# Two squared-relu layers: four plain tiles, then blocks of four tiles computed as seven half-width products

## The reference, cut to what matters

```python
def sq_relu_mlp(h, w1, w2):          # h: 512 x 1024, w1: 1024 x 4096, w2: 4096 x 1024
    u = jax.nn.relu(h @ w1)
    return (u * u) @ w2

x = x + sq_relu_mlp(rmsnorm_2(x, norm_mlp[layer]), w_mlp1[layer], w_mlp2[layer])   # layer 0 and 1
```

## Time and profile before

| what | value |
|---|---|
| median of three runs | 2443.79 us (2443.28 to 2448.42) |
| span of the profiled execution | 2446.3 us |
| its own time outside the span | not listed; the third run is 2448.42 us |
| TensorE busy | 2390.1 us (98%), 11206 matmuls |
| VectorE, ScalarE, GpSimd busy | 1234.3, 962.0, 196.0 us |
| the first layer's up tiles begin | 1483 us |
| the second layer's | 2079 us |

### The profile page before, as it was taken

How to read it: one execution, slowest core, us unless ns; L and a number is a source line. 1 busy time by engine, 2 the same in 40 slices (tenths; PEclk the granted TensorE clock), 3 DMA queues, 4 the chain that set the end, 5 groups by cost and what they waited for, 6 DMA issues and landing times.

```text
span 2446.3 us, 28445 instructions
## 1 busy us (share of the span) xinstructions
PE 2390.1 (98%) x11206; PEld 1912.1 (78%) x11206; DVE 1234.3 (50%) x2012; ACT 962.0 (39%) x1613; POOL 196.0 (8%) x147
## 2 busy tenths in 40 slices
PE   8999999999999999999999999999999899999998
PEld 7888888777777788888887677888887677888887
DVE  5533436788654445433336855424435775532432
ACT  4323224455432334322323554313324785431432
POOL 0100100322102000100100200000001100000000
PEclk9999999999999999999999999999999999999999
DMA  4323323211222232323323113322232012333332
GB/s 144 104 87 103 98 88 102 77 52 52 70 69 72 63 108 81 101 80 110 95 83 99 59 53 103 104 94 95 95 96 64 29 46 80 97 101 95 95 95 70
DMA packets 66805, 208.50 MB, mean 85 GB/s; under 512 B 7408, under 2 KB 15856, under 8 KB 66416
## 3 DMA queue, kind: packets, MB, share of 16 engines
q1 hardware_dynamic: 66672, 206.68, 27.1%
HBM read 204.55 MB, written 2.10 MB: 84 GB/s over the span
## 4 chain that ended last, share of the span: by engine, by line
PE 90%; DVE 4%; ACT 3%; issue 2%; DMA 1%; POOL 0%; POOLq 0%; SPq 0%; ACTq 0%; DVEq 0%
PE bank L1842 26%; PE bank L1846 26%; PE bank L1844 26%; PE bank L2009 2%; PE bank L1971 1%; PE bank L2016 1%; PE bank L2000 1%; PE bank L2062 1%; ACT whi L2130 1%; PE bank L1917 1%; DVE wlo L2435 1%; PE bank L1913 1%; PE bank L1915 1%; DMA wraw<-in_stream 1%; PE bank L1936 1%
## 5 line engine op out<-in xcount | busy, mean ns | idle before, releaser
L2435 DVE TENSOR_TENSOR wlo<-wraw,whi 128x1024 fp32r<-128x1024 f32 (+5 forms) x436 | 487.9, 1122 | 541.9 <-ACT whi L2130 541.1
L1842 PE MATMUL bank<-hhi,whi 128*128 128x512 f32 x1736 | 693.2, 399 | 11.4 <-ACT whi L2130 9.4
L1846 PE MATMUL bank<-hhi,wlo 128*128 128x512 f32 x1736 | 681.7, 393 | 2.1 <-DVE wlo L2435 2.1
L1844 PE MATMUL bank<-hlo,whi 128*128 128x512 f32 x1736 | 680.7, 392 | 0.4 <-DVE hlo L2442 0.4
L2130 ACT ACTIVATE whi<-wraw 128x1024 fp32r<-128x1024 f32 (+5 forms) x436 | 408.9, 940 | 493.2 <-PE bank L1846 425.0
L1842 PEld LDWEIGHTS bank<-hhi,whi 128*128 128x128 f32 x1736 | 328.1, 189 | 84.2 <-ACT whi L2130 11.4
L1846 PEld LDWEIGHTS bank<-hhi,wlo 128*128 128x128 f32 x1736 | 327.7, 189 | 74.9 <-DVE wlo L2435 5.1
L1844 PEld LDWEIGHTS bank<-hlo,whi 128*128 128x128 f32 x1736 | 328.2, 189 | 67.3 <-DVE hlo L2442 2.2
L1844 PE MATMUL bank<-mlo,whi 128*128 128x512 f32 x576 | 227.8, 395 | 0.2 <-DVE mlo L2742 0.2
L1842 PE MATMUL bank<-mhi,whi 128*128 128x512 f32 x576 | 227.8, 396 | 0.0
L1846 PE MATMUL bank<-mhi,wlo 128*128 128x512 f32 x576 | 227.7, 395 | 0.0
(11 more groups left out here) (419 smaller groups left out, 3094.7 us busy)
## 6 DMA issues: line engine op xcount, KB each, us to landing
wraw<-in_stream SPq DMA_DIRECT2D x343, 512.0 KB, 3.5
wraw<-in_stream SPq DMA_DIRECT2D x32, 192.0 KB, 2.4
wraw<-in_stream SPq DMA_DIRECT2D x22, 256.0 KB, 2.6
wraw<-in_stream SPq DMA_DIRECT2D x26, 128.0 KB, 2.0
wraw<-in_stream SPq DMA_DIRECT2D x8, 320.0 KB, 2.9
xa<-in_x SPq DMA_DIRECT2D x8, 256.0 KB, 6.4
out<-ya SPq DMA_DIRECT2D x8, 256.0 KB, 2.7
m<-in_mask SPq DMA_DIRECT2D x1, 1024.0 KB, 4.8
```

Source lines behind the costliest of these rows:

```text
L1842: pe.matmul(out, sh, xh, start=first, stop=False)
L1844: pe.matmul(out, sh, xl, start=False, stop=False)
L1846: p = pe.matmul(out, sl, xh, start=False, stop=end and last)
L2435: dve.tensor_tensor(wlo[j][:, 0:L], wraw[i][:, 0:L], whi[j][:, 0:L].bitcast(f32), SUB).then_inc(*lo.up(c))
```

## The change

Of each layer, up tiles 0 to 3 stay as they are ("plain"). The other 28 are taken in 7 blocks of four tiles (f = 4, 8, 12 in the first half; 16, 20, 24, 28 in the second). A block is a product of 512 features by 1024 channels by 512 tokens. It is cut in two along each and computed by Strassen's scheme in Winograd's form: seven products `q1`, `p5`, `p6`, `q2`, `q7`, `q4`, `q3`, each of 256 features by 512 channels by 256 tokens. Such a product is one chunk of weights: 8 weight tiles, by 3 terms, with 256 columns each, 24 matmuls.

- **Weight sums.** Of a block's four quarters `a`, `b`, `c`, `d` the sums are made in place in raw buffers: `r = c + d` by an accumulating DMA that GpSimd issues (`low`), `r += a` by VectorE (`weights_added`), `a += c` (`row`) and `r += b` (`all`) by accumulating DMAs. Raw buffers are now `wraw` (0, 1), the rotary tables' memory (2) and two more (3, 4). The split of `p5` waits for `low`, of `p6` for `weights_added`, of `q7` for `row`, of `q3` for `all`.
- **Token sums.** At the start of a layer, in four rounds k: two `plain` steps on ScalarE (gain times x), four VectorE operations of 256 columns, then a high part by ScalarE (L2436) and a low part by VectorE (L2790) of 3x256 columns. A last step (`token_last`) overwrites half of `hhi`, `hlo`.
- **Results.** Products share PSUM banks: q1, p6, q7 and q4 are added up in one, p5 and q3 in another, q2 has its own. Between products ScalarE copies the intermediate value out (`hold`), and the next product in that bank waits for the copy. VectorE adds such a copy to a bank (`corner_sum`). The four corners of a block are then cut at zero, squared and split.
- **The root.** The up results are no longer multiplied by `rb`; `rb` is squared, and each down result is multiplied by it before it is added to `ya` (`scaled_resid`), one VectorE operation more per down tile. Plain tiles are cut at zero by ScalarE.
- **Placement.** Tiles 12 to 15 of the squared values lie in `v_end`, where `xa` was.

```diff
+def products(blocks):
+    for n, blk in enumerate(blocks):
+        yield blk, "q1"
+        if n:
+            yield blocks[n - 1], "q4"
+            yield blocks[n - 1], "q3"
+        for name in ("p5", "p6", "q2", "q7"):
+            yield blk, name
...
+            lows[s].append(("acc", "low", (s, blk), r, d, None))
+            plan[c["p5"]].then = [("weights_added", (s, blk), r, a), ("acc", "row", (s, blk), a, r, None)]
+            plan[c["p6"]].then = [("acc", "all", (s, blk), r, b, c["p6"])]
...
             if half == 0:
-                ts = side_by_side(("h", s), *[(f"m{l}u0", n, 0) for n in range(3)])
-                ts.append(run(feat([(f"m{l}u0", 3, 0)], ("h", s))))
+                ts = side_by_side(("h", s), *[(f"m{l}u", n, 0) for n in range(3)])
+                afree = (*guard, *open_sums[R.next].tok)
+                token_sums(0)
+                token_sums(1)
+                ts.append(run(feat([(f"m{l}u", 3, 0)], ("h", s))))
                 R.step()
-                for f, t in enumerate(ts):
-                    square(t, f)
-                f = 4
-            while f < 16:
-                t = run(feat([(f"m{l}u{half}", half * 16 + f, 0)], ("h", s)))
-                square(t, half * 16 + f)
-                f += 1
...
+                square(ts[0], 0, afree)
+                token_sums(2)
+                square(ts[1], 1, afree)
+                token_sums(3)
+                square(ts[2], 2, afree)
+                square(ts[3], 3, afree)
+            begun = [tile(0), tile(1)]
+            h_end = multiplied(list(range(4 if half == 0 else 16, 16 + 16 * half, 4)), begun, afree)
...
+                elif k == "seven":
+                    w.wait_ge(*hi[c])
+                    waits(was)
+                    for n in range(8):
+                        xh, xl, ev_h, ev_l = quarter_of(s, name, n % 4)
+                        out = banks[b][:, 256 * (n // 4):256 * (n // 4) + 256]
+                        w.wait_ge(*ev_h)
+                        pe.matmul(out, sh, xh, start=fresh and n == 0, stop=False, skip_group_check=True)
+                        w.wait_ge(*ev_l)
+                        pe.matmul(out, sh, xl, start=False, stop=False, skip_group_check=True)
+                        w.wait_ge(*lo[c])
+                        p = pe.matmul(out, sl, xh, start=False, stop=n == 7, skip_group_check=True)
+                    p.then_inc(*used.up(c))
...
+                elif k == "acc":
+                    kind, key, r, plus, settled = a
+                    w.wait_ge(*(landed(r) if kind == "low" else added[key] if kind == "row" else lo[settled]))
+                    pool.dma_start(raw_at(r)[:, :], in_stream(plus), accum_op=ADD).then_inc(summed[kind, key][0], 16)
```

More of the change, by code:

```diff
@@ L3 @@
 from contextlib import ExitStack
[L4 removed]
+from itertools import chain as chain_of, islice
 import numpy as np
@@ L230, in split_while @@
             put("split", c)
+            for step in plan[c].then:
+                put(*step)
             state["split"] += 1
@@ L511, in ffn, with scaled_resid, residual @@
         return end
-    def residual(nxt, x, keys, hfree, k_from=0, owe=8, begun=()):
+    def scaled_resid(s, key, n, t):
+        q = T.take()
+        put("scaled_resid", s, key, n, t.bank, q.i, (t.end, *q.was), x_at[n])
+        t.freed(("combined", ("scaled", (key, n))))
+        x_at[n] = q.free = (("x_dve", (key, n)),)
+    def residual(nxt, x, keys, hfree, k_from=0, owe=8, begun=(), scaled=None):
         sx = Sum(("h", nxt))
@@ L1059, in mlp, with square, token_sums @@
     def mlp(l, s, end, nxt):
-        afree = (end, *x_at[7])
-        def square(t, f):
+        guard = (end, *x_at[7])
+        put("wide", s, guard)
+        put(*lows[s][0])
+        first, both = FT.slots
+        def square(t, f, afree):
             q = T.take()
             put("relu", s, f, t.bank, q.i, (t.end, *q.was), afree)
-            t.freed(("relu", (s, f)))
+            t.freed(("relu_sq", (s, f, "relu")))
             q.free = (("v_lo", (s, f)),)
+        def token_sums(k):
+            qs = [T.take(), T.take()]
+            for q, j in zip(qs, (k, k + 4)):
+                put("plain", s, j, q.i, (*q.was, *x_at[j]))
+            put("token_sums", s, k, qs[0].i, qs[1].i, (*first.free, *both.free), guard)
+            for q in qs:
+                q.free = (("combined", ("token", s, k, 4)),)
+            put("token_parts", s, k, guard)
+            first.free = both.free = (("p_hi", ("token", s, k)), ("p_lo", ("token", s, k)))
@@ new lines, in multiplied, with nothing @@
+        def multiplied(fs, tiles, afree):
+            def nothing():
+                pass
+            later = nothing
+            for f, name in products(fs):
+                if name == "down":
+                    next(tiles[0])
+                    next(tiles[0])
+                    later()
+                    later = nothing
+                    continue
+                at_once, then = product(f, name, afree)
+                later()
+                if (f, name) == (4, "p5"):
+                    put("token_last", s, ("used", CH[(f"m{l}u", 3, 0)]))
+                at_once()
+                later = then
+            next(tiles[1])
+            next(tiles[1])
+            later()
+            return ("used", CH[(f"m{l}s", fs[-1], "q3")])
@@ new lines, in program, with ready_at, in_stream @@
+        summed = {}
+        for k, *a in steps:
+            if k == "acc":
+                sums_of[a[0]] += 1
+                summed[a[0], a[1]] = s_sum[a[0]], 16 * sums_of[a[0]]
+        def ready_at(chunk):
+            if not chunk.ready:
+                return landed(chunk.raw)
+            kind, key = chunk.ready
+            return added[key] if kind == "both" else summed[kind, key]
+        def in_stream(r):
+            return t["stream"][r.place:r.place + 128 * r.size()].rearrange("(p l) -> p l", p=128)
```

385 lines of the change are left out of this document (316 added, 69 removed).

## The result

| | median us | runs | ratio to before (95%) |
|---|---|---|---|
| before | 2444.77 (2443.11 to 2448.86) | 20 | |
| after | 2450.72 (2448.70 to 2455.66) | 20 | 1.0026 [1.0020, 1.0032] |

The change makes the kernel about 6 us slower (5.95 by the medians, 6.4 by the ratio), where 12.4 were forecast; 2450.7 lies in the range and, 1.7 us above its lower edge, in the forecast's own range of 2449 to 2466. The profiled execution of after took 2451.38 us, its span is 2449.6.

The account below looks back on a forecast made before the run. TensorE's matmuls were taken as the bound; -22.4 products, +3.4 operand memory, +27.2 layer starts, +3.0 clock and +1.2 root made +12.4 us on 2443.8, so 2456 us, range 2436 to 2485.

Parts of the forecast that it names:

- The bound: Squared-relu layers: they wait only for TensorE's own matmuls, so any new wait of TensorE is paid in full.
- The products: Blocks of four up tiles: 168 matmuls at 0.1200 us replace 96 at 0.2267, 1.60 us less a block, 22.4 in 14.
- where the operands lie: p5, p6, q7 read token sums in the layer's slower memory: half the excess assumed, +3.4 us; `v_end` taken as 0.
- The start of a layer: Token rounds and squares queue on ScalarE and VectorE; p6 waits for q1's copy: 13.6 us a layer, 27.2 us.
- the clock: After TensorE's stand at each layer's start, some matmuls run at 1.2 GHz: 3.0 us for both layers.
- The steady state: Later blocks: ScalarE and VectorE fit; TensorE waits only if an accumulating DMA takes over 8.5 us from start to landing.
- The accumulating DMA: Weight sums: landing in 6 us, costed at nothing; DMA engines could sustain 4.5 us of engine time for each.
- The root at the residual: One more VectorE operation per down tile, hidden except at each layer's last tile: 0.6 us each, together 1.2.
- Rival 1: Layer starts: token rounds run back to back with squares beside them, TensorE loses 4.9 us a layer: 2436 us; chance 0.11.
- The bound of 0.2%: What a measurement can tell from no change, 4.9 us: faster is below 2438.9, slower above 2448.7 us.

Follow-up runs that it names:

- experiments 1 to 3: After, with token rounds early and plain tiles' squares late: 2430.35 us; without token rounds, results wrong: 2435.93 us; with only the token rounds early: 2442.58 us.
- experiment 4: After, with the weight sum `row` done twice, the second once the first has landed, so q7's weights are wrong: 2518.80 us, ratio 1.0300.
- experiment 5: After, with GpSimd's DMAs writing over the buffer instead of adding, so the weights are not the sums: 2450.76 us, ratio 1.0019.

## Why the prediction was right

- *The bound.* Right: the new waits of TensorE are all at the two starts, and each was paid in full.
- *The products* (-22.4) *and where the operands lie* (+3.4), together -19.0: measured 2 x (-12.5 - 0.65) = -26.3. The 0.1200 of the earlier trace rows held to 0.0001 us. The mis-sized term is the second, by 7 us: the token sums' matmuls are at 0.1179, under h's and not above, and `v_end` gained 1.3 us where 0 was taken (1.3 a layer was the upper bound). Why a 256-column matmul on the token sums is the faster one is open.
- *The start of a layer* (+27.2) *and the clock* (+3.0), together +30.2: measured 15.4 + 14.6 = 30.0. p6 is 14.45 and 13.6 us late, 28.1 for the 27.2 of the start. The half clock behind p6 is the rest, 1.9 for 3.0: in the first layer the clock is back at 1.00 when p6 starts, since most of p5 ran at half clock while p6 had to wait for q1's copy anyway. The order of ScalarE's queue gave this, with round 3's high part and q1's copy as its two last links, and experiments 1 to 3 show both links and each one's share.
- *The steady state.* Right: no wait of a later block; experiment 4 finds the cover at 7.1 to 8.5 us, where 8.5 was forecast.
- *The accumulating DMA* (0, landing in 6 us). Right, and experiment 5 finds no price for the addition. Its engine time is 3.1 us, less than the bound of 4.5. One reading was off: the first `low` was given 7.6 us and took 8.9, so ScalarE waited 1.5 us, without a cost in the layer. The Trainium skill's price for a DMA from GpSimd ("DMA: Bandwidth & Descriptors", section "Anatomy of one DMA — SWDGE (gpsimd) path"), by which 512 KB are an estimated 3.2 us, now has a row beside it: 3.9 us for a plain one, and 6.2 for one that adds, a case which the formula doesn't tell apart.
- *The root at the residual* (+1.2): mis-sized. At the same clock the tail of after is 0.2 us longer than before, not 0.6; the 0.6 of the first layer can't be told from the scatter there.

The sum was +12.4, and the medians have +6.0. The operand memory and `v_end` are 7.3 us of error in one direction, the root's term up to 1 in the same; 2 to 3 us outside the layers, which no term had, go the other way and stay open. That the time still lay inside the forecast's own range is in part luck, as these errors go against each other. Rival 1 was wrong on after as built, and came near once the rounds and squares were moved: a start then costs 4.4 and 7.4 us, where the rival has 4.9. The bound of 0.2% (4.9 us) was passed narrowly, by 1.1 us by the medians and 1.5 by the ratio.

## What to carry to other kernels

A scheme that saves arithmetic on the bounding engine pays only if its preparation fits in the other engines' idle time, in the order of their queues: here 26 us saved were spent, and 4 more, on two starts where ScalarE had work in line that nobody needed yet. Walk the queue of the helping engine row by row to the last link that the bounding engine asks for, and not only to the one that the profile names: that one hides the next. And compare a rewritten kernel with the old one after both have had the same cheap repairs, such as an aligned buffer.

## What the runs showed of the hardware

- A 512-column fp32r matmul whose moving operand starts 32 bytes past a multiple of 64 costs 4.4 ns more from start to start (f1a: 233.5 to 229.1 ns; m in before: 233.3 to 228.9). Padding one buffer by 32 bytes is worth 11.5 to 14 us in both kernels. The 256-column matmuls of the token sums showed nothing of it (117.9 ns either way).
- A stand of TensorE costs more than its length: after 2.6 us of it the granted clock was 0.50 and 0.69 for the next 4 us, 1.7 us of work; ten stands of 3.4 to 6.0 us, 45.7 together, made two layers 67 us longer (experiment 4).
- An accumulating DMA of 512 KB takes twice a plain one's engine time (5.3% against 2.7% of the span for 42 of them) and 2.3 us longer to land.
- The same unchanged work between the layers, with waits within 0.5 us, took 3.75 us less in one execution than in the other, at another granted clock; a comparison of two single spans can't be trusted below that.
